# Gate and up projections of a 512-token layer by one level of Strassen's scheme on half of the contraction

## The reference

```python
def swiglu(h, w1, w3, w2):
    return (jax.nn.silu(h @ w1) * (h @ w3)) @ w2

h = rmsnorm(x, g_ffn1[l])
x = x + 0.5 * swiglu(h, w1_a[l], w3_a[l], w2_a[l])
...                                        # mixing block
h = rmsnorm(x, g_ffn2[l])
x = x + 0.5 * swiglu(h, w1_b[l], w3_b[l], w2_b[l])
return rmsnorm(x, g_final)
```

## Time and profile before

| | us |
|---|---|
| median of 3 runs | 1155.24 (1151.45 to 1155.61) |
| the profiled execution's own time | 1158.78 |
| span of its trace | 1157.0 |
| PE busy | 1128.4 |
| PEld busy (beside PE) | 922.3 |
| DVE busy | 622.9 |
| ACT busy | 423.5 |

### The profile page before, as it was taken

How to read it: one execution, slowest core, us unless ns; L and a number is a source line. 1 busy time by engine, 2 the same in 40 slices (tenths; PEclk the granted TensorE clock), 3 DMA queues, 4 the chain that set the end, 5 groups by cost and what they waited for, 6 DMA issues and landing times.

```text
span 1157.0 us, 13715 instructions
## 1 busy us (share of the span) xinstructions
PE 1128.4 (98%) x5086; PEld 922.3 (80%) x5094; DVE 622.9 (54%) x875; ACT 423.5 (37%) x604; POOL 0.2 (0%) x4
## 2 busy tenths in 40 slices
PE   7999999999999999998899999999999999999996
PEld 6888888888888878877677788888888888888885
DVE  6644335433458768776666555666443354433454
ACT  6323123222233466665655433423232133222231
POOL 0000000000000000000000000000000000000000
PEclk9999999999999999998999999999999999999998
DMA  8232232332323212111111133422332222322211
GB/s 281 93 109 91 91 109 75 107 97 86 100 70 121 92 37 73 37 55 55 37 55 33 32 99 94 145 91 91 110 104 96 91 95 86 109 91 91 91 55 73
DMA packets 32878, 102.63 MB, mean 89 GB/s; under 512 B 4160, under 2 KB 5568, under 8 KB 32832
## 3 DMA queue, kind: packets, MB, share of 16 engines
q1 hardware_dynamic: 32832, 102.01, 27.1%
HBM read 99.90 MB, written 2.10 MB: 88 GB/s over the span
## 4 chain that ended last, share of the span: by engine, by line
PE 89%; DVE 5%; ACT 3%; issue 2%; DMA 0%; DVEq 0%; SPq 0%; ACTq 0%
PE acc L938 28%; PE acc L940 28%; PE acc L939 27%; ACT rope L511 1%; PE pair_bank L938 1%; PE bank L946 1%; DVE w_lo L640 1%; PE bank L948 1%; PE pair_bank L940 1%; PE pair_bank L939 1%; DVE ebuf L819 1%; DVE spA_hi L824 0%; DVE x L931 0%; PE bank L1118 0%; DMA w_raw<-in_w13a 0%
## 5 line engine op out<-in xcount | busy, mean ns | idle before, releaser
L938 PE MATMUL acc<-xg_hi,w_hi 128*128 128x512 f32 x1008 | 400.4, 397 | 7.2 <-DVE w_lo L752 7.2
L940 PE MATMUL acc<-xg_hi,w_lo 128*128 128x512 f32 x1008 | 394.9, 392 | 0.0
L939 PE MATMUL acc<-xg_lo,w_hi 128*128 128x512 f32 x1008 | 394.7, 392 | 0.0
L640 DVE TENSOR_TENSOR w_lo<-w_raw,w_hi 128x1024 fp32r<-128x1024 f32 (+3 forms) x194 | 218.3, 1143 | 52.1 <-ACT w_hi L430 48.3
L430 ACT ACTIVATE w_hi<-w_raw 128x1024 fp32r<-128x1024 f32 (+3 forms) x194 | 186.6, 987 | 132.8 <-PE acc L940 132.6
L938 PEld LDWEIGHTS acc<-xg_hi,w_hi 128*128 128x128 f32 x1008 | 191.0, 189 | 48.5 <-issue 8.4
L940 PEld LDWEIGHTS acc<-xg_hi,w_lo 128*128 128x128 f32 x1008 | 190.7, 189 | 41.0
L939 PEld LDWEIGHTS acc<-xg_lo,w_hi 128*128 128x128 f32 x1008 | 191.1, 190 | 39.3 <-issue 0.7
L938 PE MATMUL acc<-hid_hi,w_hi 128*128 128x512 f32 x352 | 138.7, 394 | 0.0
L940 PE MATMUL acc<-hid_hi,w_lo 128*128 128x512 f32 x352 | 138.0, 392 | 0.0
L939 PE MATMUL acc<-hid_lo,w_hi 128*128 128x512 f32 x352 | 136.6, 388 | 0.0
(11 more groups left out here) (166 smaller groups left out, 950.2 us busy)
## 6 DMA issues: line engine op xcount, KB each, us to landing
w_raw<-in_w13b SPq DMA_DIRECT2D x44, 512.0 KB, 3.3
w_raw<-in_w13a SPq DMA_DIRECT2D x40, 512.0 KB, 3.3
w_raw<-in_wmix SPq DMA_DIRECT2D x22, 512.0 KB, 3.2
w_raw<-in_w2a SPq DMA_DIRECT2D x16, 512.0 KB, 3.6
w_raw<-in_w2b SPq DMA_DIRECT2D x16, 512.0 KB, 3.6
w_raw<-in_wgate SPq DMA_DIRECT2D x8, 512.0 KB, 3.2
w_raw<-in_wend SPq DMA_DIRECT2D x8, 512.0 KB, 3.5
w_raw<-in_wo SPq DMA_DIRECT2D x8, 512.0 KB, 3.3
```

The costliest lines, as they stand in the source:

```text
L640: dve.tensor_tensor(w_lo[:, s, 0:width], w_raw[:, s, 0:width], w_hi[:, s, 0:width].bitcast(F32), ALU.subtract).then_inc(wlo_done, 1)
L938: pe.matmul(o, w_h, r_h, start=first, stop=False, skip_group_check=check)
L939: pe.matmul(o, w_h, r_l, start=False, stop=False, skip_group_check=check)
L940: return pe.matmul(o, w_l, r_h, start=False, stop=last, skip_group_check=check)
```

## The change

For 20 of the 22 pairs of each feed-forward block (all but the first two, `PLAIN`) the upper half of the contraction, blocks 0 to 3 of 8, is no longer multiplied out in full. Gate and up tile, the two halves of those four blocks and the two halves of the tokens make a 2 x 2 by 2 x 2 block product. It takes 7 block products in place of 8; each is `quarter_products`: 2 blocks x 3 matmuls of 256 columns. Blocks 4 to 7 stay as they were (`rest_of_unit`, 12 matmuls of 512 columns for each of the two units).

For this, four sums of the activations are made and split once for each feed-forward block (`sums_operands`, `t_hi` and `t_lo`), and four sums of the weights for each pair (`weight_sums`, `s_raw`, then `s_hi` and `s_lo`); of the up unit only blocks 2 to 7 are still split (`split_second_hi`, `split_second_lo`). Partial results pass from one quarter of the banks to another: `first_product` (P1) goes to a bank of its own, from which ScalarE seeds two quarters (`seed_first`); P6 is accumulated on one of them, copied negated to the third quarter (semaphore `seed2`), P7 is accumulated on top and copied to the fourth (`seed3`); P5 goes to a second spare bank, is copied to SBUF and is added to two quarters by VectorE before it takes the pair (`take_pair`). The engines' orders for a pair are in the new `fast_pair` functions. A load into a slot now waits for the weight sums as well. The loops over pairs are written out. The first two down units are worked through in halves, 0, 1, 0, 1.

The diff, cut to its core, 8 spaces of indentation taken off, lines taken out not shown (they are the printed `up_pair` and loops):

```diff
...
 EPS = 1e-6
 NEG = -1e30
 RING = 4
+Q = 2
+QW = Q * P
+HALF = SEQ // 2
+PLAIN = 2
+FAST = NF - PLAIN
...
...
+def fast_index(u0):
+    for b, base in enumerate((FFN_A, FFN_B)):
+        for c, (f0, n) in enumerate(CHUNKS):
+            f = f0 + (u0 - chunk_base(base, c)) // 2
+            if f0 <= f < f0 + n and u0 >= chunk_base(base, c) and f >= PLAIN:
+                return b * FAST + f - PLAIN
+    return None
+bank_p1, bank_p5 = bank[1][:, 0:HALF], bank[2][:, 0:HALF]
+def quarters(u0):
+    o1, o2 = acc[u0 % RING], acc[u0 % RING + 1]
+    return o1[:, 0:HALF], o1[:, HALF:SEQ], o2[:, 0:HALF], o2[:, HALF:SEQ]
...
         s = u0 % RING
         if u0 >= RING:
             wait_lo(sp, u0 - RING, i)
+            if fast_index(u0 - RING) is not None:
+                sp.wait_ge(s_made, 4 * (fast_index(u0 - RING) + 1))
         sp.dma_start(w_raw[:, s, 0:src.shape[-1]], src).then_inc(w_loaded[s], 16)
...
+    def sums_operands(b):
+        for m in range(2 * Q):
+            act.activation(xgf[:, m, :], x[:, m, :], ACT.Copy,
+                           scale=gains[:, 2 * b, m:m + 1]).then_inc(xgf_done, 1)
+        for t in range(2):
+            act.wait_ge(tsum_done, 4 * b + 2 * t + 2)
+            act.activation(t_hi[:, 2 * t:2 * t + 2], tsum[:, 2 * t:2 * t + 2], ACT.Copy).then_inc(t_hi_done, 1)
+    def split_second_hi(u):
+        s, g = u % RING, fast_index(u)
+        act.wait_ge(w_loaded[s], 16 * (u // RING + 1))
+        act.wait_ge(unit_done, u - RING + 1)
+        act.activation(w_hi[:, s, QW:KD * P], w_raw[:, s, QW:KD * P], ACT.Copy).then_inc(whi_done, 1)
+        act.wait_ge(s_made, 4 * (g + 1))
+        act.activation(s_hi[:, g % 2], s_raw[:], ACT.Copy).then_inc(s_hi_done, 1)
+    def seed_first(u):
+        g = fast_index(u)
+        r1, r3, r4, r2 = quarters(u)
+        act.wait_ge(p1_done, g + 1)
+        act.wait_ge(acc_read[u % RING], reads(u, 0))
+        act.wait_ge(acc_read[(u + 1) % RING], reads(u + 1, 0))
+        act.activation(r1, bank_p1, ACT.Copy).then_inc(seed1, 1)
+        act.activation(r2, bank_p1, ACT.Copy, scale=-1.0).then_inc(seed1, 1)
...
+    def plain_pairs(base, fb, n_norm):
+        for j in range(PLAIN):
             u = base + 2 * j
...
+            if n_norm == 0 and j == 0:
+                sums_operands(0)
+                split_hi(RING, 0, KD * P)
+            elif j == 0:
+                split_hi(u + 2, 0, KD * P)
+                split_hi(u + 3, 0, KD * P)
+                sums_operands(1)
+            else:
+                if n_norm:
+                    split_hi(RING + base, 0, KD * P)
+                split_second_hi(RING + base + 1)
+                seed_first(RING + base)
+            if j == 0:
                 rms(n_norm)
                 act.preload_act_table_set("silu_and_others")
...
+            silu(u, fb + j)
+            hidden_hi(fb + j, j)
+    def fast_pair(u, f, slot, first, last):
+        g = fast_index(u)
+        r1, r3, r4, r2 = quarters(u)
+        act.wait_ge(p6_done, g + 1)
+        act.activation(r3, r2, ACT.Copy, scale=-1.0).then_inc(seed2, 1)
+        act.wait_ge(p5_done, g + 1)
+        if g:
+            act.wait_ge(p5_added, 2 * g)
+        act.activation(p5, bank_p5, ACT.Copy).then_inc(p5_copied, 1)
+        split_hi(u + 2, 0, unit_width(u + 2))
+        act.wait_ge(p7_done, g + 1)
+        act.activation(r4, r2, ACT.Copy).then_inc(seed3, 1)
+        if not first:
+            silu(u - 2, f - 1)
+        if last:
+            split_hi(u + 3, 0, unit_width(u + 3))
+        else:
+            split_second_hi(u + 3)
+        if not first:
+            hidden_hi(f - 1, slot - 1)
+        if last:
+            silu(u, f)
+            hidden_hi(f, slot)
+        else:
+            seed_first(u + 2)
...
             u += 2 * n
             for m in range(KD):
...
+                if m == KD - 1 and c < len(CHUNKS) - 1:
+                    split_second_hi(u + m + 2)
+                    seed_first(u + m + 1)
+                elif u + m + 2 < UNITS:
                     split_hi(u + m + 2, 0, unit_width(u + m + 2))
                 if c == len(CHUNKS) - 1:
                     if m == 0:
...
+    def sums_operands(b):
+        first, second = xgf[:, 0:Q, :], xgf[:, Q:2 * Q, :]
+        b11, b12 = first[:, :, 0:HALF], first[:, :, HALF:SEQ]
+        b21, b22 = second[:, :, 0:HALF], second[:, :, HALF:SEQ]
+        dve.wait_ge(xgf_done, 2 * Q * (b + 1))
+        dve.tensor_tensor(tsum[:, 0], b12, b11, ALU.subtract).then_inc(tsum_done, 1)
+        dve.wait_ge(tsum_done, 4 * b + 1)
+        dve.tensor_tensor(tsum[:, 1], b22, tsum[:, 0], ALU.subtract).then_inc(tsum_done, 1)
+        dve.tensor_tensor(tsum[:, 2], b12, b22, ALU.subtract).then_inc(tsum_done, 1)
+        dve.wait_ge(tsum_done, 4 * b + 2)
+        dve.tensor_tensor(tsum[:, 3], b21, tsum[:, 1], ALU.subtract).then_inc(tsum_done, 1)
+        dve.wait_ge(tsum_done, 4 * b + 4)
+        for t in range(2):
+            dve.wait_ge(t_hi_done, 2 * b + t + 1)
+            dve.tensor_tensor(t_lo[:, 2 * t:2 * t + 2], tsum[:, 2 * t:2 * t + 2],
+                              t_hi[:, 2 * t:2 * t + 2].bitcast(F32), ALU.subtract).then_inc(t_lo_done, 1)
+    def weight_sums(u):
+        g, s1, s2 = fast_index(u), u % RING, u % RING + 1
+        dve.wait_ge(w_loaded[s1], 16 * (u // RING + 1))
+        dve.wait_ge(w_loaded[s2], 16 * (u // RING + 1))
+        if g:
+            dve.wait_ge(s_hi_done, g)
+            dve.wait_ge(s_lo_done, g)
+        a11, a12 = w_raw[:, s1, 0:QW], w_raw[:, s1, QW:2 * QW]
+        a21, a22 = w_raw[:, s2, 0:QW], w_raw[:, s2, QW:2 * QW]
+        dve.tensor_tensor(s_raw[:, 0], a21, a22, ALU.add).then_inc(s_made, 1)
+        dve.tensor_tensor(s_raw[:, 2], a11, a21, ALU.add).then_inc(s_made, 1)
+        dve.wait_ge(s_made, 4 * g + 1)
+        dve.tensor_tensor(s_raw[:, 1], s_raw[:, 0], a11, ALU.add).then_inc(s_made, 1)
+        dve.wait_ge(s_made, 4 * g + 3)
+        dve.tensor_tensor(s_raw[:, 3], s_raw[:, 1], a12, ALU.add).then_inc(s_made, 1)
+    def split_second_lo(u):
+        s = u % RING
+        dve.wait_ge(whi_done, u + 1)
+        dve.wait_ge(unit_done, u - RING + 1)
+        dve.tensor_tensor(w_lo[:, s, QW:KD * P], w_raw[:, s, QW:KD * P], w_hi[:, s, QW:KD * P].bitcast(F32),
+                          ALU.subtract).then_inc(wlo_done, 1)
+    def split_sums_lo(u):
+        g = fast_index(u)
+        dve.wait_ge(s_hi_done, g + 1)
+        dve.wait_ge(s_made, 4 * (g + 1))
+        dve.tensor_tensor(s_lo[:, g % 2], s_raw[:], s_hi[:, g % 2].bitcast(F32),
+                          ALU.subtract).then_inc(s_lo_done, 1)
+    def take_pair(u, f):
+        g = fast_index(u)
+        if g is None:
+            dve.wait_ge(unit_done, u + 1)
+        else:
+            r1, r3, r4, r2 = quarters(u)
+            dve.wait_ge(unit_done, u + 2)
+            dve.wait_ge(p5_copied, g + 1)
+            dve.tensor_tensor(r3, r3, p5, ALU.subtract).then_inc(p5_added, 1)
+            dve.tensor_tensor(r2, r2, p5, ALU.add).then_inc(p5_added, 1)
+            dve.wait_ge(p5_added, 2 * g + 1)
+        dve.tensor_tensor(gate[:, f % 2, :], acc[u % RING][:], rstd[:],
+                          ALU.mult).then_inc(acc_read[u % RING], 1)
+        if g is None:
+            dve.wait_ge(unit_done, u + 2)
+        else:
+            dve.wait_ge(p5_added, 2 * g + 2)
+        dve.tensor_tensor(up[:, f % 2, :], acc[u % RING + 1][:], rstd[:],
+                          ALU.mult).then_inc(acc_read[u % RING + 1], 1)
...
+    def plain_pairs(base, fb, n_norm):
+        for j in range(PLAIN):
             u = base + 2 * j
...
+            if n_norm == 0 and j == 0:
+                sums_operands(0)
+                split_lo(RING, 0, KD * P)
+            elif j == 0:
+                split_lo(u + 2, 0, KD * P)
+                split_lo(u + 3, 0, KD * P)
+                sums_operands(1)
+            else:
+                if n_norm:
+                    split_lo(RING + base, 0, KD * P)
+                weight_sums(RING + base)
+                split_second_lo(RING + base + 1)
+                split_sums_lo(RING + base)
+            if j == 0:
                 norm(n_norm)
...
+            take_pair(u, fb + j)
+            multiply(u, fb + j)
+            hidden_lo(fb + j, j)
+    def fast_pair(u, f, slot, first, last):
+        if not first:
+            take_pair(u - 2, f - 1)
+        split_lo(u + 2, 0, unit_width(u + 2))
+        if not last:
+            weight_sums(u + 2)
+        if not first:
+            multiply(u - 2, f - 1)
+        if last:
+            split_lo(u + 3, 0, unit_width(u + 3))
+        else:
+            split_second_lo(u + 3)
+            split_sums_lo(u + 2)
+        if not first:
+            hidden_lo(f - 1, slot - 1)
+        if last:
+            take_pair(u, f)
+            multiply(u, f)
+            hidden_lo(f, slot)
...
+                if m == KD - 1 and c < len(CHUNKS) - 1:
+                    weight_sums(u + m + 1)
+                    split_second_lo(u + m + 2)
```

(135 more changed lines are left out.)

59 lines of the change are left out of this document (28 added, 31 removed).

## The result

The changed kernel takes 1159.09 us (median of 20 runs, 1157.38 to 1161.01), the one before 1155.91 us in the same job (20 runs, 1151.19 to 1159.62): ratio 1.0023, interval 1.0013 to 1.0033. Forecast was +2.7 us; measured is +3.2 by the medians (+2.7 by the ratio), or 1158 forecast against 1159.1. An eighth of the matmul work in half of the contraction of 40 pairs is gone, and the kernel is a shade slower.

A forecast was written before the change was run, and what follows sets the result against it. TensorE, busy 98% of the span with 89% of the chain of waits, was taken as the bound. -20.2 + 3.8 + (10.1 + 1.0) + (5.5 + 2.5) = +2.7 us, median 1158 us; range 1146 to 1171.

The forecast's parts named there:

- 40 pairs by seven products: Feed-forward pairs on TensorE: 10.38 us in place of 10.88, 0.50 us saved a pair, 20.2 us in all.
- copy before P7, steady state: P7 waits for ScalarE's copy of P6, not fully hidden by P5: 0.10 us a pair, 38 times, 3.8 us.
- first block's start without clock: First feed-forward block: TensorE waits 8.5 us for s_lo, then for the copy before P7; 10.1 us late.
- clock, first block: TensorE's clock falls after the 8.5 us stop; range 0 to 3.4 us, 1.0 taken.
- second block's start without clock: Second feed-forward block: TensorE waits 4.0 us for unit 4's split, then for the copy before P7; 5.5 us late.
- clock, second block: TensorE's clock falls after the 4.0 us stop and meets dense work; range 0 to 3.4 us, 2.5 taken.
- everything else: Added steady-state work, loads, chunk ends, the mixing block and written-out down units: nothing.
- Both rivals on the distance: 256-column matmuls: at the load floor, 1141 us (faster case, chance 0.15); or bare weight loads, some 1340 us (chance 0.02).
- load floor of 0.11 us: Least distance of short matmuls, set by the weight load; reaching it would save 33 us over the pairs.
- the rival rested that I gave a quarter: Before P7 in each pair: copy dearer or ScalarE late, up to 0.37 us a pair, 1168 us; chance 0.25.
- Slack of VectorE and written-out loops: Steady-state pairs: added VectorE work is free while under 1.3 us late; written-out matmuls follow without gaps: nothing.

The follow-up runs named there:

- double copy: The changed kernel with the copy of P6 that P7 waits for done twice in each of 40 pairs; ratio to the kernel before 1.0125.
- the filled stop: The changed kernel with 30 matmuls of 512 columns, result unused, in the first block's stop of TensorE; ratio to the kernel before 1.0025.
- plain8: The changed kernel with each block's first 8 pairs left plain and the activation sums made during the fourth pair; 1144.35 us, ratio to before 0.9902.

## Why the prediction was right

Step by step, forecast against measured:

| term | forecast us | measured us |
|---|---|---|
| 40 pairs by seven products | -20.2 | -16.4 |
| copy before P7, steady state | +3.8 | 0 |
| first block's start without clock | +10.1 | +10.1 |
| clock, first block | +1.0 | +1.0 |
| second block's start without clock | +5.5 | +4.9 |
| clock, second block | +2.5 | 0 |
| everything else | 0 | +3.6 (what is left) |
| sum | +2.7 | +3.2 (by the medians) |

**The gain.** The mechanism was right and the size 19% off. Two distances were mis-sized, the short one because four matmuls were the sample, the long one because it was taken from a stream of long ones alone: 0.1175 became 0.1187 (42 x 0.0012 = 0.05 us a pair), and 0.2267 became 0.2284 next to short ones (24 x 0.0017 = 0.04 us a pair). Both rivals on the distance fell. The load floor of 0.11 us was not reached, and no load stands bare: 118.7 ns from one short matmul to the next, load included. The rule of the Trainium skill ("TensorE: Matmul & The Clock Gate", section "The mechanism") that loads of the same rows don't overlap a running matmul doesn't hold in this kernel; the same section elsewhere also lets loads into a background weight buffer run ahead, and no run here tells whether that is what happens.

**The copy.** Each part was priced right (end of P6, 0.04 us, 0.37 us) but for the last: the stream resumes 0.16 us behind the copy's end (double copy) and not 0.23, and P5 with its slightly longer distances covers 1.42. So the wait is nil. That the chain has no slack, on which the rival rested that I gave a quarter, is shown by the double copy: 0.30 us for each pair. The rival was well founded; the price was 0.1 us a pair too high. The beat came out as forecast with the wait (10.48) because this error and the distances' cancel.

**The first start.** Right, 11.1 us forecast and measured, and by the steps given: `xgf`, the four subtractions, `split_lo`, norm, weight sums, `s_lo` at 42.1 (41.7 forecast), P7 at 45.09 (44.95). The argument didn't need the amount of VectorE's work (64% busy) but its order at the one place where it isn't ahead. The 1.0 us for the clock is the difference behind P7 between the filled stop and the empty one; that it meets the forecast exactly is in part luck, since I had taken it from a range of 0 to 3.4 us.

**The second start.** Stops of 3.4 and 1.3 us for 4.0 and 1.5, from stream to stream. Unit 4's split was ready 0.4 us sooner than I had it: 807.06 is 14.25 us behind the start of unit 1's stream (792.81), forecast 802.9 - 788.24 = 14.66. The clock didn't fall there, against my 2.5 us: a stop of 4 us in otherwise dense work isn't the mixing block's stretch with a third of its time idle, from which I had it. Why one brings the clock down and the other does not is open.

**The rest.** By the traces: 17.1 us in place of 13.7 at a granted 0.50 in the mixing block (half of the difference, 1.7 us, lost, an estimate), 44.0 in place of 44.8 us for the w_o units (-0.8), 0.1 us more in each of the four groups of down units behind which a fast pair comes (0.4), 0.3 us at the very start. This is +1.6. By the traces, whose spans differ by 1.6, the rest comes to 2.0; by the medians, which differ by 3.2, to 3.6. The difference is within what single executions vary, and part of it has a cause on record. Of 46 executions of the kernel before in the later jobs, 13 had a mean granted clock of 0.994 to 0.996 and took 1151.3 to 1153.5 us, 33 had 0.987 to 0.992 and took 1155.6 to 1159.4. All 20 of the changed kernel had 0.983 to 0.986. The profiled execution of `plain8`, at 0.994, shows where: it was at 0.50 for some 3 us of the mixing block, the one of before, at 0.989, for 13.7. So how often the clock falls in the mixing block moves a single execution by about 5 us, and no term of the sum had it. What decides it isn't shown. I had "nothing" for all of this. Slack of VectorE and written-out loops: nothing forecast, nothing measured, each with a run of its own.

So the sum was right partly because errors cancelled: the gain came out 3.8 us short and the rest 3.6 us dear, while the copy (3.8), the second block's clock (2.5) and its start (0.6) were priced too high. That 2.7 and 3.2 us lie so close is luck. What carried the verdict were the two starts, 16.0 us given back of 16.4 gained.

## What to carry to other kernels

Work that a cleverer algorithm adds for the feeding engines is free where they are ahead and is paid in full where they aren't: read the starts and seams of a kernel by their order, step by step, before the average load. Then leave the scheme out where it would stop the bound engine (here the first pairs of each block, where it brought a gain of 1.0 to 1.3%). A chain of result, copy and next product across two engines has to be covered by other matmuls; price it to 0.05 us if it recurs in each iteration.
